# A float32r matmul stream read backwards in two alternating halves, and activation buffers moved by 128 bytes

## The reference

```
first block:  h = x + gla(rmsnorm(x))            # 4 heads, two directions, chunked gated linear attention
              h = h + swiglu(rmsnorm(h))         # 2048 -> 2 x 5632 -> 2048
              h = rmsnorm(h + sigmoid(rmsnorm(h) @ w_gate) * (p @ w_proj))
second block: proj = rmsnorm(h) @ w_in           # 2048 -> 16400: q, k, v, gates, pool input
              mLSTM with 8 heads, multi-scale pooling, two gated branches
              y = h + rmsnorm(merged @ w_out)
```

## Time and profile before

| | |
|---|---|
| median of 3 runs | 2201.73 us (2200.83 to 2202.91) |
| the profiled execution's own time | 2200.2 us |
| its span, first to last instruction | 2198.5 us |
| TensorE stream (PE) busy | 2188.7 us, 9954 matmuls |
| TensorE weight load (PEld) busy | 1819.9 us |
| VectorE busy | 1574.8 us |
| ScalarE busy | 1082.1 us |
| HBM traffic | 410 MB read, 188 GB/s |
| granted TensorE clock | 1.00 of 2.4 GHz |

### The profile page before, as it was taken

One profiled execution on the slowest core, in us unless ns is written; L12 is line 12 of the kernel. 1 busy time (PEld: TensorE's weight loads), 2 busy tenths in 40 slices (PEclk: granted clock), 3 DMA queues, 4 the chain that ended last, 5 costly groups with the idle time before them and its releaser, 6 DMA issues.

```text
span 2198.5 us, 27733 instructions
## 1 busy us (share of the span) xinstructions
PE 2188.7 (100%) x9954; PEld 1819.9 (83%) x9954; DVE 1574.8 (72%) x2395; ACT 1082.1 (49%) x1369; POOL 19.8 (1%) x41
## 2 busy tenths in 40 slices
PE   9999999999999999999999999999999999999998
PEld 8888888888888888888888888888888888888887
DVE  6887888877776457777778846889455559645875
ACT  5564554544444334444446545555445555443443
POOL 0000000000000000000000000000000000000000
PEclk9999999999999999999999999999999999999999
DMA  9654566666666666666666656666665556666663
GB/s 281 182 163 122 179 196 189 200 192 195 194 193 192 192 195 191 196 191 194 186 217 198 200 152 191 183 199 181 201 176 171 171 162 205 196 195 211 191 192 114
DMA packets 282925, 413.96 MB, mean 188 GB/s; under 512 B 21071, under 2 KB 145883, under 8 KB 282299
## 3 DMA queue, kind: packets, MB, share of 16 engines
q1 hardware_dynamic: 281806, 408.55, 61.9%
q10 hardware_dynamic: 1008, 3.94, 0.5%
HBM read 410.33 MB, written 2.10 MB: 188 GB/s over the span
## 4 chain that ended last, share of the span: by engine, by line
PE 99%; issue 0%; DMA 0%; DVE 0%; ACT 0%; DVEq 0%; POOLq 0%; POOL 0%; SPq 0%; ACTq 0%
PE acc L1314 31%; PE acc L1316 31%; PE acc L1315 31%; PE mx L1494 1%; PE mx L1535 0%; PE tp L1362 0%; DMA H<-in_x 0%; PE tp L1508 0%; PE tp L1507 0%; PE tp L1509 0%; PE mx L1291 0%; PE mx L1293 0%; PE mx L1292 0%; PE mx L1472 0%; PE tp L1552 0%
## 5 line engine op out<-in xcount | busy, mean ns | idle before, releaser
L1686 DVE TENSOR_TENSOR w_lo<-raw,w_hi 128x1024 fp32r<-128x1024 f32 (+1 forms) x769 | 934.9, 1219 | 524.5 <-ACT w_hi L801 520.7
L801 ACT CAST w_hi<-raw 128x1024 fp32r<-128x1024 f32 (+1 forms) x769 | 803.0, 1046 | 913.9 <-PE acc L1316 897.0
L1314 PE MATMUL acc<-w_hi,xa_hi 128*128 128x512 f32 x2228 | 874.8, 393 | 0.0
L1316 PE MATMUL acc<-w_hi,xa_lo 128*128 128x512 f32 x2228 | 867.4, 389 | 0.0
L1315 PE MATMUL acc<-w_lo,xa_hi 128*128 128x512 f32 x2228 | 867.2, 389 | 0.0
L1316 PEld LDWEIGHTS acc<-w_hi,xa_lo 128*128 128x128 f32 x2228 | 418.2, 188 | 87.8
L1314 PEld LDWEIGHTS acc<-w_hi,xa_hi 128*128 128x128 f32 x2228 | 418.5, 188 | 84.8
L1315 PEld LDWEIGHTS acc<-w_lo,xa_hi 128*128 128x128 f32 x2228 | 418.6, 188 | 84.2
L1314 PE MATMUL acc<-w_hi,xb_hi 128*128 128x512 f32 x384 | 149.6, 390 | 0.0
L1316 PE MATMUL acc<-w_hi,xb_lo 128*128 128x512 f32 x384 | 149.4, 389 | 0.0
L1315 PE MATMUL acc<-w_lo,xb_hi 128*128 128x512 f32 x384 | 149.4, 389 | 0.0
(11 more groups left out here) (313 smaller groups left out, 1240.4 us busy)
## 6 DMA issues: line engine op xcount, KB each, us to landing
raw<-in_w_in SPq DMA_DIRECT2D x192, 512.0 KB, 3.8
raw<-in_ffn_w_in SPq DMA_DIRECT2D x352, 256.0 KB, 2.9
raw<-in_gla_w_in SPq DMA_DIRECT2D x95, 512.0 KB, 4.0
raw<-in_ffn_w_out SPq DMA_DIRECT2D x88, 512.0 KB, 3.7
raw<-in_w_in SPq DMA_DIRECT2D x128, 256.0 KB, 3.0
raw<-in_gla_w_out SPq DMA_DIRECT2D x32, 512.0 KB, 4.1
raw<-in_ple_w_gate SPq DMA_DIRECT2D x32, 512.0 KB, 4.0
raw<-in_w_proj_mlstm SPq DMA_DIRECT2D x32, 512.0 KB, 3.7
```

Of the source, the lines that this page charges most:

```text
L801: nc.scalar.copy(w_hi[:, hl, 0:kc * job.w], raw[:, slot, 0:kc * job.w]).then_inc(hi_ready, 1)
L1314: nc.tensor.matmul(a[t][:, 0:w], xh, hi, start=first, stop=False)
L1316: ins = nc.tensor.matmul(a[t][:, 0:w], xl, hi, start=False, stop=last)
L1686: nc.vector.tensor_tensor(w_lo[:, hl, 0:kc * job.w], raw[:, slot, 0:kc * job.w], w_hi[:, hl, 0:kc * job.w].bitcast(F32), ALU.subtract) \
```

## The change

The moving operand and the output of the three matmuls of `product` are viewed as two halves of 256 columns, each in 32 pieces of 8 columns. The stream takes the last piece of the first half backwards, the last piece of the second half backwards, then the piece before it of the first half, and so on. Operand and output have the same order, so each result is written to the same place as before. The view is used in `product` only, not in the other products listed above.

The activation buffers start 128 bytes later: `used_to[0] += P` stands ahead of `xa_hi`, and the three alignments follow `xa_at` in place of `w_hi_at`. So every stationary operand of `product` begins 128 bytes past the place, within 512 bytes, of the weight slots. All other tensors behind `xa_hi` move along. To make room, the scratch area reserved at the start of SBUF is set to 8192 bytes, half its default of 16384; every SBUF tensor therefore lies 8192 bytes lower.

```
         w_lo, _ = own("w_lo", [P, HL_SLOTS, 2 * NC], F32R, HL_SLOTS * 4096)
+        used_to[0] += P
         xa_hi, xa_at = own("xa_hi", [P, 16, T], F32R, 16384)
...
-        o += (w_hi_at - o) % NC
+        o += (xa_at - o) % NC
         A_hi = at("A_hi", [P, 4, P], F32R, o); o += 2048
...
-        hid_at = phase + (w_hi_at - phase) % NC
+        hid_at = phase + (xa_at - phase) % NC
...
-        o += (w_hi_at - o) % NC
+        o += (xa_at - o) % NC
         yb_hi = at("yb_hi", [P, 8, T], F32R, o)
...
-                        nc.tensor.matmul(a[t][:, 0:w], xh, hi, start=first, stop=False)
-                        nc.tensor.matmul(a[t][:, 0:w], xh, lo, start=False, stop=False)
-                        ins = nc.tensor.matmul(a[t][:, 0:w], xl, hi, start=False, stop=last)
+                        to, high, low = streamed(a[t][:, 0:w]), streamed(hi), streamed(lo)
+                        nc.tensor.matmul(to, xh, high, start=first, stop=False)
+                        nc.tensor.matmul(to, xh, low, start=False, stop=False)
+                        ins = nc.tensor.matmul(to, xl, high, start=False, stop=last)
...
+            def streamed(tile):
+
+                return tile.rearrange("p (h b c) -> p b h c", h=2, c=8)[:, ::-1, :, ::-1]
...
-    nc = bacc.Bacc("TRN2", target_bir_lowering=False, num_devices=1)
+    nc = bacc.Bacc("TRN2", target_bir_lowering=False, num_devices=1, dynamic_dma_scratch_size=8192)
```

## The result

The changed kernel takes 2359.3 us (median of 4 runs, 2358.49 to 2359.65), the kernel before 2201.28 us in the same session. The ratio is 1.0717, with a 95% interval of 1.0698 to 1.0735: 158 us slower, where I had forecast 97 us faster. The profiled execution of the changed kernel has a span of 2356.8 us.

A forecast was written before the change was run, and what follows sets the result against it. TensorE's own matmul pace was taken as the bound: 2200.2 - 99.0 for the cleared pace + 1.0 for late elementwise work = 2102.2 us profiled, so 2104 us median; range 2080 to 2205 us, slower case left out.

The forecast's parts named there:

- What bounds the kernel: Whole span: only TensorE's own pace sets the time; 9084 matmuls at 226.7 ns make 2059 us, 94% of the span.
- Readings of the 13.4 ns: Loss of each 512-column matmul over 213.3 ns: four readings of trace rows, mostly toward weight load and moving operand clashing.
- the clash is gone: Matmuls of `product`: if SBUF is divided by address within 512 bytes, new order and offset end the load-stream clash.
- the gain of 10.9 ns a matmul: Matmuls of `product`: pace falls from 226.7 to 215.8 ns, the plain float32 rows' value; 99.0 us over 9084.
- The walk in step: Load and moving operand in `product` both advance 32 bytes in 6.7 ns; 128 bytes keep them from meeting.
- The clue of the earlier trace: Same instructions behind four small transposes go at 232 ns, then 225 ns; taken to show that phase matters.
- The alternation of pieces: Stream of `product`: changing halves every 8 columns costs nothing; bounds zero and 10 ns a matmul, 93 us.
- The output order: PSUM writes of `product` in the new order: taken to cost nothing, though the Trainium skill speaks against non-contiguous patterns.
- The backward step: Stream of `product` read last to first: taken to cost nothing; halved rate, about 4020 us, held as remote.
- The other products: 180 matmuls of opening product, embedding, pooling and attention output, order kept: at most 2.4 us either way, taken as zero.
- Slower: each change of piece costs: Rival, chance 0.20: in `product`, 64 changes cost 0.16 ns each, 2295 us; a clock each, 2345 or 2444 us.
- No change: Rival, chance 0.13: the loss lies in the reading port or float32r, not addresses; 2202 us within 4 us.

The follow-up runs named there:

- p1: Kernel before with only the 128-byte offset and the smaller scratch area, stream in its old order: 2250.95 us, ratio 1.0226.
- p12: Kernel before with smaller scratch area, tensors at their old addresses, but raw, w_hi and w_lo 128 bytes lower: 2250.56 us, ratio 1.0226.
- p2: Kernel before with only the new order of the stream, activation buffers and scratch area unchanged (offset 0): 2418.99 us, ratio 1.0991.
- p3: Changed kernel with its pieces of 8 columns taken from two halves by turns, but first to last and forward: 2349.27 us, ratio 1.0674.
- p6: Changed kernel with the moving operand read forward and contiguously, only the output written in the new order: 2250.46 us.
- p11: Kernel before with only the scratch area of 8192 bytes, every tensor 8192 bytes lower: 2200.6 us, ratio 0.9999.
- p4: Changed kernel with all 512 columns last to first and no alternation of halves: 2265.64 us, ratio 1.0294.
- q3: Kernel before with 128-byte offset; stream goes forward over pieces of 8 columns, each read backward, no second half: 2261.69 us.
- p9: Changed kernel with pieces of 16 columns (64 bytes) in place of 8: 2200.52 us.
- p7: Changed kernel with one activation column used for all 128 stationary columns (step zero): 2356.3 us.
- p10: Changed kernel with pieces of 4 columns (16 bytes) in place of 8: 2437.65 us.
- p8: Kernel before with one activation column used for all 128 stationary columns: 2237.41 us.
- q7: Changed kernel with pieces of 16 columns, backward, offset 128, and one activation column for all 128 stationary columns: 2198.13 us.

## Why the prediction was wrong

**What bounds the kernel** was right: TensorE's pace in 9084 matmuls is where the time went, 156.5 us of 158.3 in the trace. The sums of the prediction come out right; what failed are the values put into them.

**Readings of the 13.4 ns.** The reading that the two streams get in each other's way and that addresses within a few hundred bytes matter was right in kind: the 128 bytes alone are worth 50 us in the old order (p1, p12) and 60 us with the opposite sign in the new one (p2 against the changed kernel). The step that failed first is the one from there to the sum: "the clash is gone", that is, that the 13.4 ns were the price which the new order would take away. No arrangement took any of it away in the steady stream of 512 columns: the kernel before stood at the best pace that any of these kernels reached, and every other arrangement tried either kept it or added to it. Of the gain of 10.9 ns a matmul nothing came; a loss of 17.4 was measured. The walk in step, which I worked out from the speed of the load, did not do what it was meant to do. With it, the two should have met all the time without the offset and never at 128 bytes. What was found is 24.0 ns of cost at 0 and 17.4 at 128: the right order, but no clash cleared. And the walk forward in the same pieces, which can't be in step if the backward one is, costs 1.1 ns less than the backward one (p3). The clue of the earlier trace rows was read rightly, though its second figure is rounded: the steps there settle at 226 to 227 ns, not 225, so it showed a worse phase than the usual one and never a better one.

**"The alternation of pieces ... cost nothing by my reading"** is the second step that failed, and it carries most of the loss: from p1 to the changed kernel it is 108 us, 11.9 ns a matmul. I took it from the earlier trace rows, where runs of 8 from two regions cost nothing, and reasoned that the number of clocks for each run is what counts. Those rows differ from the new order in two ways: they are float32, two clocks a column, and they never come back for the other 8 of 16 columns in a region. At one column a clock, pieces of 8 columns taken from two halves cost 11.9 ns backward and 10.8 forward (p3 against p1), and pieces of 16 nothing backward but 7.5 forward. The bound of the prediction, 0.16 ns for each of 64 changes, 10 ns, is close to the 11.9 measured by luck: 64 turns in place cost 1.2 ns, and 32 changes of half cost nothing backward.

**The output order** was rightly priced at nothing (p6 against p1), and so was the smaller scratch area (p11). The backward step was priced at nothing and costs 1.6 ns a matmul at this offset (p4 against p1). **The offset** was to remove a clash; in the old order it costs 5.5 ns (p1, p12).

**The other products** were given at most 2.4 us either way; the pooling product moved by at most 1.3 ns for each of 48, which is nothing in the sum.

**The rivals.** "Slower: each change of piece costs" was the right side and named the reader that fetches beyond the 32 bytes and throws part away. Its numbers were 2295 us with the clash left and the price of the short runs, and 2345 to 2444 at a clock a change. That 2359 lies between them is luck, as its fixed price for each change is refuted (q3, p9). "No change" put the loss down to the reading port or to float32r; the steady 13.4 ns may still be that, but the time did not stay. The Trainium skill's rule that TensorE never waits on anyone (SBUF — State Buffer, Who interferes with whom) is not what these runs show: with instructions, shapes and waits the same, the distance between two buffers moves the time by 2.3% (p12).

**What stays open.** Which read meets which. Meeting at fixed places within 256 bytes would fit the offsets, but not that the changed order costs the same with one loaded address (p7). That the load and the stream are each read in blocks of 64 bytes, and that a second fetch of a block takes time that the load needs, fits p9, q3 and p10 in direction; it was argued and not shown, and it does not say why forward pieces of 16 cost 13.0 ns where backward ones cost nothing. Nor is it shown what the 13.4 ns of the kernel before are. A run of the stream with no weight load at all would tell most, but each matmul here brings its own load, and it was not tried.

## What to carry to other kernels

A float32r matmul stream at one column a clock is sensitive to where its two operands stand and to how the moving one is walked. Here the plain order at a distance of 0 or 256 bytes was never beaten. Keep that, or test any other arrangement by itself before a second one is put on top. A pattern's price at half rate need not be its price at full rate. Before a row is used against a reading, make sure which load runs beside which stream. A fixed loss per instruction is not a gain to be had until some arrangement shows a smaller one.

## What was not expected of the hardware

- In the plain order, an offset of 128 bytes between stationary and moving operand adds 5.5 ns to 226.7, 64 bytes add 6.3, and 256 bytes nothing.
- Taking the moving operand in 32-byte pieces from two halves raises the time of a matmul to between 243 and 251 ns, in 16-byte pieces to 253 ns; in 64-byte pieces it ranges from 226.7 to 239.7 ns with offset and direction.
- Writing a PSUM bank in pieces of 32 bytes from two halves, backward, costs nothing at a pace of 232 ns: 2250.46 us against 2250.95 with a contiguous output.
- A stationary operand with a step of zero slows the plain stream at offset 0 by 4.0 ns a matmul (p8) and moves the other two orders by 3 us or less (p7 against the changed kernel, q7 against p9).
- The pooling product, with the same addresses and instructions, goes at 118.7 ns in p1 and 120.0 ns in p4, after a different order of the stream before it.
